# Output matrix: the first two blocks over the seven ready tiles, their low parts two merges ahead; feed-forward: convolution before the low parts, silu behind the first high part

## The chip, the cores and the metric

The program runs on one core of one Trainium2 chip. The metric is the device time in microseconds (us) of one execution, from three timed runs. Engines: PE is TensorE (matmul), DVE is VectorE, ACT is ScalarE, POOL is GpSimd, SP only issues DMAs.

## The reference, cut to what matters

A hybrid mixer block with a feed-forward part, and behind it a second block of another kind. The change touches these lines of the first block, on 256 positions and a model width of 1024:

```python
merged = (gates[:, :, 0] * (y_a @ sc_out) + gates[:, :, 1] * (y_b @ sb_out)
          + gates[:, :, 2] * (y_c @ rw_out) + gates[:, :, 3] * (y_d @ sg_out))
x = x + merged @ w_o
h = rms_norm(x, ffn_norm_g)
up = causal_dwconv(h @ w_up, conv_w)          # 3 taps, 2 * 2816 columns
gate, val = jnp.split(up, 2, axis=-1)
x = x + (jax.nn.silu(gate) * val) @ w_down
```

Everything is float32. Channels lie on partitions: a tile is 128 channels by 256 positions, and the width of 1024 is KT = 8 tiles.

## The kernel before, in words

**Weights and the split.** All weights come as one stream of blocks, 128x1024 floats (512 KB) each, through a ring of 8 slots. SP issues one DMA for each block, in order, once the slot's last reader is done. A float32 product is made of three fast ones: ACT copies a block rounded (the high part, `part_high` L254, in the feed-forward `ff_high` L1074), DVE subtracts (the low part, `part_low` L258, in the feed-forward `ff_low` L1079), and PE makes three 128x256 matmuls for each of the block's 8 pieces, 24 for a block (`three`, L263 to L265; in the feed-forward L1254 to L1256 in `up` and L1266 to L1268 in `down`).

**The merge and the output matrix (W_O).** PE first makes the branch products (`branches`, L1102), 8 blocks. For each of the 8 output tiles k DVE merges: `merge_one` (L1175, L1177), the low part of the tile before (`merged_lower(k - 1)`, L1181), two additions (L1194, L1195). ACT rounds the merged tile (L1132). Then W_O: 8 blocks m = 0..7, each a sum over the 8 merged tiles k. Its block m needs its own low part, and at m = 0 each piece k waits until tile k is merged, rounded and subtracted. DVE makes the low part of block 0 behind merge 6 (ahead of merge 7), and that of block 1 behind merge 7, ahead of `merged_lower(7)`. ACT makes the high parts of blocks 0, 1, 2 behind the roundings of tiles 3, 4, 5.

**The feed-forward.** 2816 channels are 22 tiles, each with two blocks of `w_up` (gate and value; `up`, two blocks of PE work) and one of `w_down` (`down`, one block). Two tiles (j = 0, 1) are a round of the loop; a loop of `pairs` = 10 rounds does `up` for the tiles two behind those of `down`, and two pairs of `up` stand ahead of it. Between `up` and `down` of a tile stand, on DVE, `scale_up` (L1293, twice, which also frees the PSUM banks), `convolve` (L1303 twice, L1306 four times); on ACT the silu (L1347); on POOL `hide` (L1377, L1379, L1383: product, high part, low part). `hide(i, j)` overwrites the operands of `down` of the round before, so it waits until that one has ended. In each half j of a round DVE did: low part of block 0, scale, low part of block 1, convolution, low part of block 2; ACT did three high parts and then the silu. Names below: block (n, i) is block n = 0..5 of round i; block (0, 10) and block (1, 10) are the two last ones, both of `w_down`. Nothing reorders instructions: each engine runs its own list in the written order, and the engines are tied by semaphores alone. Behind the stage stands a barrier of all engines.

## Time and profile before

| | |
|---|---|
| three timed runs | 1650.66, 1651.3, 1653.53 us; median 1651.3 |
| the profiled execution | 1651.11 us, its span 1649.3 us |
| PE busy in the span | 1587.9 us (96%) |
| DVE, ACT, POOL busy | 1180.9 us (72%), 827.8 us (50%), 435.5 us (26%) |
| mean granted clock of PE | 0.987 of full speed |

Read it so: PE is busy nearly all the time, so only the places where it stands still, or runs at a lower clock, can give time back to a change that leaves PE's work as it is. Times in rows are us from the start of the span.

### The profile page before, as it was taken

Reading aid. Unit: us, or ns where it says so; the run is one execution under the profiler, and the core shown is the slowest. Engines: PE = TensorE matmul, PEld = TensorE weight load, DVE = VectorE, ACT = ScalarE, POOL = GpSimd, SP = SyncE. Lnnn points to the kernel's source line nnn. Section 1 sums busy time; section 2 is a strip of 40 time slices with the busy share of each in tenths; the row PEclk is TensorE's granted clock in tenths of the full one; section 3 lists DMA queues with packets and bytes.
Section 4 is the critical chain, followed back from the end, with each engine's and each line's share of the span. In section 5 each row is a group of like instructions: output and inputs, shape, how many; then the busy total and the mean of one; then the engine's idle time right before and its main releaser. Section 6 shows DMA issues by size and latency. Waiting matters only on the chain. (4 is left out here: it accounts for less than half of the span.)

```text
span 1649.3 us, 34054 instructions
## 1 busy us (share of the span) xinstructions
PE 1587.9 (96%) x11842; PEld 1462.3 (89%) x11842; DVE 1180.9 (72%) x2295; ACT 827.8 (50%) x1357; POOL 435.5 (26%) x261
## 2 busy tenths in 40 slices
PE   7997999999998999999999999999999999999997
PEld 7987987999998977789999999999999888888886
DVE  5666326687786877716699996777774777777776
ACT  5364334455554463233556454555555555555554
POOL 1245540044441003456668990000000000000000
PEclk9988999999999999999999999999999999999999
DMA  8522444356663421155558775655557777777763
GB/s 288 158 62 82 127 142 128 128 180 183 186 215 118 167 77 52 59 176 197 157 170 234 217 221 165 176 177 176 182 177 223 245 241 240 232 237 238 239 227 123
DMA packets 92812, 289.56 MB, mean 176 GB/s; under 512 B 10304, under 2 KB 27072, under 8 KB 92352
## 3 DMA queue, kind: packets, MB, share of 16 engines
q1 hardware_dynamic: 92304, 287.61, 55.3%
q8 instruction: 52, 0.85, 0.2%
q10 hardware_dynamic: 432, 0.90, 0.2%
q14 instruction: 24, 0.20, 0.0%
HBM read 270.65 MB, written 17.83 MB: 175 GB/s over the span
## 5 line engine op out<-in xcount | busy, mean ns | idle before, releaser
L265 PE MATMUL psum<-arena_parts,ring_parts 128*128 128x256 f32 (+1 forms) x1856 | 525.2, 283 | 0.0
L263 PE MATMUL psum<-arena_parts 128*128 128x256 f32 (+2 forms) x1664 | 479.4, 288 | 26.5 <-DVE ring_parts L258 11.7
L2756 DVE TENSOR_TENSOR ring_parts<-ring,arena_parts 128x512 fp32r<-128x512 f32 x418 | 282.7, 690 | 112.8 <-ACT arena_parts L2550 94.8
L265 PEld LDWEIGHTS psum<-arena_parts,ring_parts 128*128 128x128 f32 x1856 | 356.0, 192 | 0.0
L263 PEld LDWEIGHTS psum<-arena_parts 128*128 128x128 f32 x1664 | 316.3, 190 | 29.5 <-DVE ring_parts L258 10.7
L264 PE MATMUL psum<-h_parts,arena_parts 128*128 128x256 f32 x1024 | 287.1, 280 | 0.0
L258 POOL TENSOR_TENSOR ring_parts<-ring,arena_parts 128x1024 fp32r<-128x1024 f32 x79 | 209.7, 2677 | 67.7 <-ACT arena_parts L254 48.8
L2519 PE MATMUL psum<-arena_parts,x_parts 128*128 128x512 f32 x512 | 201.4, 393 | 0.8 <-DVE x_parts L2783 0.8
L2520 PE MATMUL psum<-ring_parts,x_parts 128*128 128x512 f32 x512 | 201.7, 394 | 0.0
L2521 PE MATMUL psum<-arena_parts,x_parts 128*128 128x512 f32 x512 | 201.4, 393 | 0.0
L264 PEld LDWEIGHTS psum<-h_parts,arena_parts 128*128 128x128 f32 x1024 | 194.4, 190 | 0.0
L2550 ACT ACTIVATE arena_parts<-ring 128x512 fp32r<-128x512 f32 x209 | 131.5, 629 | 113.3 <-PE psum L2521 94.6
L2547 ACT ACTIVATE arena_parts<-ring 128x512 fp32r<-128x512 f32 x209 | 131.7, 630 | 69.8 <-PE psum L2521 57.3
L264 PE MATMUL psum<-arena_parts 128*128 128x256 f32 (+1 forms) x576 | 164.5, 286 | 0.0
L2519 PEld LDWEIGHTS psum<-arena_parts,x_parts 128*128 128x128 f32 x512 | 96.0, 187 | 23.6 <-DVE ring_parts L2756 1.0
L2520 PEld LDWEIGHTS psum<-ring_parts,x_parts 128*128 128x128 f32 x512 | 96.2, 188 | 22.4
L2521 PEld LDWEIGHTS psum<-arena_parts,x_parts 128*128 128x128 f32 x512 | 96.5, 188 | 21.4
L1079 DVE TENSOR_TENSOR ring_parts<-ring,arena_parts 128x1024 fp32r<-128x1024 f32 x66 | 85.7, 1301 | 38.4 <-ACT arena_parts L1074 33.7
L264 PEld LDWEIGHTS psum<-arena_parts 128*128 128x128 f32 x576 | 110.5, 192 | 0.2
L352 POOL TENSOR_TENSOR ring_parts<-ring,rounded 128x1024 fp32r<-128x1024 f32 x32 | 79.5, 2492 | 114.7 <-ACT rounded L254 114.6
L254 ACT ACTIVATE arena_parts<-ring 128x1024 fp32r<-128x1024 f32 x76 | 78.7, 1054 | 60.2 <-DMA ring<-stream 60.2
L1074 ACT ACTIVATE arena_parts<-ring 128x1024 fp32r<-128x1024 f32 x66 | 69.3, 1058 | 65.0 <-DMA ring<-stream 64.8
(547 smaller groups left out, 3270.3 us busy)
## 6 DMA issues: line engine op xcount, KB each, us to landing
ring<-stream SPq DMA_DIRECT2D x473, 512.0 KB, 3.7
kept<-arena SPq DMA_DIRECT2D x128, 128.0 KB, 2.0
arena<-kept SPq DMA_DIRECT2D x32, 512.0 KB, 4.5
arena<-first SPq DMA_DIRECT2D x1, 2144.0 KB, 16.7
arena<-second SPq DMA_DIRECT2D x1, 1632.0 KB, 6.6
x<-x_t SPq DMA_DIRECT2D x1, 1024.0 KB, 5.5
out<-arena SPq DMA_DIRECT2D x4, 256.0 KB, 2.1
arena<-last ACTq DMA_DIRECT2D x1, 512.0 KB, 3.4
```

Of the source, the lines that this page charges most:

```text
L258: ns.tensor_tensor(low[:, s, :], ring[:, s, :], high[:, s, :].bitcast(F32), ALU.subtract)\
L263: nc.tensor.matmul(dst, stationary[0], moving[0], start=first, stop=False)
L264: nc.tensor.matmul(dst, stationary[0], moving[1], start=False, stop=False)
L265: return nc.tensor.matmul(dst, stationary[1], moving[0], start=False, stop=last_one)
L352: ns.tensor_tensor(low[:, g % 4, :], ring[:, g % 4, :], rounded[:, g % 4, :].bitcast(F32), ALU.subtract)\
L1079: nc.vector.tensor_tensor(low[:, s, :], ring[:, s, :], high[:, s, :].bitcast(F32), ALU.subtract)\
L2519: mm(b, gate_high[:, q % 4, t], expert_high[:, m % 2, w], start=False, stop=False)
L2520: mm(b, gate_high[:, q % 4, t], low[:, s, w], start=False, stop=False)
L2521: ins = mm(b, gate_low[:, q % 4, t], expert_high[:, m % 2, w], start=False, stop=last_one)
L2547: nc.scalar.activation(expert_high[:, m % 2, halves[0]], ring[:, s, halves[0]], ACT.Copy)\
L2550: nc.scalar.activation(expert_high[:, m % 2, halves[1]], ring[:, s, halves[1]], ACT.Copy)\
L2756: v.tensor_tensor(low[:, s, w], ring[:, s, w], expert_high[:, m % 2, w].bitcast(F32), ALU.subtract)\
```

## The change

In W_O, PE takes blocks 0 and 1 over the tiles 0 to 6 first, then tile 7 of both, and then the blocks 2 to 7 as before. DVE makes the low part of block 0 behind merge 4 and that of block 1 behind merge 6, so that none stands behind merge 7. In the feed-forward, DVE does in each half of a round scale, convolution and then the three low parts; ACT does the silu behind the first of the three high parts. In the last round of the loop PE does both `up` and then both `down`. The last two halves are put together likewise on DVE (scale, convolution, low part) and ACT (high part, silu). The numbers of matmuls, vector operations and DMAs are the same.

```diff
+                def onto(m, ks):
+                    s, b = W_O[m], m % 4
+                    if ks[0] == 0:
+                        pe.wait_ge(full[s], (pe_at.rounds[s] + 1) * 16)
+                        pe.wait_ge(drained[b], pe_at.banks[b] + m // 4 + 1)
+                        pe.wait_ge(S("low"), o_base + m + 1)
+                    for k in ks:
+                        if m == 0 or k == KT - 1:
+                            pe.wait_ge(S("merged"), k + 1)
...
-                project(pe, W_O[:4], range(4), 1, onto(0))
-                project(pe, W_O[4:], range(4), 1, onto(4))
+                for m in range(2):
+                    onto(m, range(KT - 1))
+                for m in range(2):
+                    onto(m, range(KT - 1, KT))
+                for m in range(2, KT):
+                    onto(m, range(KT))
...
-                        if k == 6:
-                            weights_low(0)
-                weights_low(1)
+                        if k in (4, 6):
+                            weights_low(k // 2 - 2)
                 merged_lower(KT - 1)
...
-                with pe.Fori(0, pairs) as i:
+                with pe.Fori(0, pairs - 1) as i:
                     for j in range(2):
                         up(3 * j, i)
                         down(3 * j + 2, i, j)
+                for j in range(2):
+                    up(3 * j, pairs - 1)
+                for j in range(2):
+                    down(3 * j + 2, pairs - 1, j)
...
                     for j in range(2):
-                        ff_low(dve, 3 * j, i)
                         scale_up(i, j)
-                        ff_low(dve, 3 * j + 1, i)
                         convolve(i, j)
-                        ff_low(dve, 3 * j + 2, i)
-                for j in range(2):
-                    ff_low(dve, j, pairs)
-                for j in range(2):
-                    scale_up(pairs, j)
-                    convolve(pairs, j)
+                        for part in range(3):
+                            ff_low(dve, 3 * j + part, i)
+                scale_up(pairs, 0)
+                convolve(pairs, 0)
+                ff_low(dve, 0, pairs)
+                scale_up(pairs, 1)
+                convolve(pairs, 1)
+                ff_low(dve, 1, pairs)
...
                         ff_high(act, 3 * j, i)
+                        silu(i, j)
                         ff_high(act, 3 * j + 1, i)
                         ff_high(act, 3 * j + 2, i)
-                        silu(i, j)
                 for j in range(2):
                     ff_high(act, j, pairs)
-                for j in range(2):
                     silu(pairs, j)
```

DVE at the last merges, before, from the last addition of merge 6 on. L258 is a low part of W_O, L1175 and L1177 open a merge, L1181 is the low part of a merged tile, L1194 and L1195 are the additions:

```order
L1195 TENSOR_TENSOR arena<-arena 128x256
L258 TENSOR_TENSOR ring_parts<-ring,arena_parts 128x1024
L1175 TENSOR_TENSOR arena<-psum,arena 128x512
L1177 TENSOR_TENSOR arena<-psum,arena 128x512
L1181 TENSOR_TENSOR arena_parts<-arena,arena_parts 128x256
L1194 TENSOR_TENSOR arena<-arena 128x512
L1195 TENSOR_TENSOR arena<-arena 128x256
L258 TENSOR_TENSOR ring_parts<-ring,arena_parts 128x1024
L1181 TENSOR_TENSOR arena_parts<-arena,arena_parts 128x256
```

The same place of the change, from the last addition of merge 6 on (lines are 9 higher: L1184 for L1175, L1186 for L1177, L1190 for L1181, L1203 and L1204 for the additions):

```order
L1204 TENSOR_TENSOR arena<-arena 128x256
L258 TENSOR_TENSOR ring_parts<-ring,arena_parts 128x1024
L1184 TENSOR_TENSOR arena<-psum,arena 128x512
L1186 TENSOR_TENSOR arena<-psum,arena 128x512
L1190 TENSOR_TENSOR arena_parts<-arena,arena_parts 128x256
L1203 TENSOR_TENSOR arena<-arena 128x512
L1204 TENSOR_TENSOR arena<-arena 128x256
L1190 TENSOR_TENSOR arena_parts<-arena,arena_parts 128x256
L258 TENSOR_TENSOR ring_parts<-ring,arena_parts 128x1024
```

The low part between the last addition and the last L1181 is gone; the L258 ahead of merge 7 is now that of block 1, and that of block 0 stands two merges earlier.

DVE at the head of the feed-forward's loop, before (L1079 a low part, L1293 the scaling, L1303 and L1306 the convolution; the other rows are register work):

```order
L1079 TENSOR_TENSOR ring_parts<-ring,arena_parts 128x1024
L1292 REGISTER_ALU
L1293 TENSOR_TENSOR arena<-psum,scale 128x256 x2
L1078 REGISTER_ALU
L1079 TENSOR_TENSOR ring_parts<-ring,arena_parts 128x1024
L1297 ISA
L1302 ISA
L1303 ISA
L1303 TENSOR_SCALAR arena<-arena,par 128x256
```

The head of the same loop in the change, where L1305 is the scaling, L1315 and L1318 are the convolution:

```order
L1329 ISA
L1305 TENSOR_TENSOR arena<-psum,scale 128x256 x2
L1309 ISA
L1314 ISA
L1315 ISA
L1315 TENSOR_SCALAR arena<-arena,par 128x256
L1314 REGISTER_ALU
L1315 ISA
L1315 TENSOR_SCALAR arena<-arena,par 128x256
```

Scale and convolution no longer have low parts ahead of or between them.

PE where the feed-forward's loop ends, before, with what each row waits for (L1266 to L1268 are `down`):

```order
L1268 MATMUL psum<-arena_parts,ring_parts 128x256
L1273 REGISTER_ALU
L1273 COMPARE_AND_BRANCH
L1266 MATMUL psum<-arena_parts 128x256 [waits ff_hidden,low]
L1267 MATMUL psum<-arena_parts 128x256
L1268 MATMUL psum<-arena_parts,ring_parts 128x256
```

The same place of the change (L1274 to L1276 are `down`, L1262 to L1264 are `up`):

```order
L1276 MATMUL psum<-arena_parts,ring_parts 128x256
L1281 REGISTER_ALU
L1281 COMPARE_AND_BRANCH
L1262 MATMUL psum<-arena_parts 128x256 [waits low,up_taken]
L1263 MATMUL psum<-h_parts,arena_parts 128x256
L1264 MATMUL psum<-arena_parts,ring_parts 128x256
```

Behind the loop's end now stand four blocks of `up` and then four of `down`; before there were two of `down`, and the loop had one round more.

## Rows read from the trace of the kernel before

**Rows 1.** Windows; columns PE, PEld, DVE, ACT, POOL busy, clock, DMA share, GB/s

```profile
338.06:340.00 1.94, 1.94 (x9) 1.94 (x10) 1.93 (x6) 0.00 (x0) 0.00 (x0) 0.50 0.12 46
342.00:500.00 158.00, 158.00 (x1346) 158.00 (x1346) 126.45 (x209) 88.18 (x92) 66.74 (x57) 1.00 0.62 191
515.00:519.00 4.00, 4.00 (x22) 4.00 (x21) 4.00 (x8) 2.98 (x5) 0.00 (x0) 0.57 0.50 210
```

**Rows 2.** Timeline of PE, W_O: start, duration, instruction, [idle before, releaser]

```profile
288.58 0.35 PE L263 MATMUL psum<-arena_parts 128*128 128x256 f32 x1 [0.97 <-DVE ring_parts L258]
...
292.69 0.38 PE L263 MATMUL psum<-arena_parts 128*128 128x256 f32 x1 [1.40 <-DVE arena_parts L1181]
```

**Rows 3.** Timeline of PE, feed-forward: first down, two ups, last down

```profile
338.06 0.58 PE L1266 MATMUL psum<-arena_parts 128*128 128x256 f32 x1 [2.90 <-POOL arena_parts L1383]
...
342.29 0.28 PE L1254 MATMUL psum<-arena_parts 128*128 128x256 f32 x1
...
494.68 0.28 PE L1254 MATMUL psum<-arena_parts 128*128 128x256 f32 x1
...
507.32 0.36 PE L1266 MATMUL psum<-arena_parts 128*128 128x256 f32 x1 [1.19 <-POOL arena_parts L1383]
```

**Rows 4.** Timeline of DVE at the merges 5, 7 and behind

```profile
280.80 0.69 DVE L1175 TENSOR_TENSOR arena<-psum,arena 128x512 f32<-128x512 f32 x1 [0.65 <-PE psum L1102]
...
287.10 1.23 DVE L258 TENSOR_TENSOR ring_parts<-ring,arena_parts 128x1024 fp32r<-128x1024 f32 x1
288.24 0.68 DVE L1175 TENSOR_TENSOR arena<-psum,arena 128x512 f32<-128x512 f32 x1
...
289.56 0.41 DVE L1181 TENSOR_TENSOR arena_parts<-arena,arena_parts 128x256 fp32r<-128x256 f32 x1
...
291.07 1.22 DVE L258 TENSOR_TENSOR ring_parts<-ring,arena_parts 128x1024 fp32r<-128x1024 f32 x1
292.22 0.42 DVE L1181 TENSOR_TENSOR arena_parts<-arena,arena_parts 128x256 fp32r<-128x256 f32 x1
```

**Rows 5.** Timeline of ACT at the loop's start (high parts, table load, silu)

```profile
324.88 1.06 ACT L1074 ACTIVATE arena_parts<-ring 128x1024 fp32r<-128x1024 f32 x1 [2.61 <-DMA ring<-stream]
327.95 1.06 ACT L1074 ACTIVATE arena_parts<-ring 128x1024 fp32r<-128x1024 f32 x1 [2.02 <-DMA ring<-stream]
330.62 1.06 ACT L1074 ACTIVATE arena_parts<-ring 128x1024 fp32r<-128x1024 f32 x1 [1.61 <-DMA ring<-stream]
331.70 1.28 ACT L1347 ACT_TABLE_LOAD   x1
333.00 0.42 ACT L1347 ACTIVATE arena<-arena 128x256 f32<-128x256 f32 x1
```

**Rows 6.** Timeline of DVE at the loop's start (scale, convolution)

```profile
327.11 0.75 DVE L1293 TENSOR_TENSOR arena<-psum,scale 128x256 f32<-128x256 f32 x2
...
330.19 0.61 DVE L1303 TENSOR_SCALAR arena<-arena,par 128x256 f32<-128x256 f32 x2
330.71 1.70 DVE L1306 SCALAR_TENSOR_TENSOR arena<-arena,par 128x255 f32<-128x255 f32 x4
```

**Rows 7.** Timeline of POOL: the first hide and the last two

```profile
333.59 0.85 POOL L1377 TENSOR_TENSOR arena<-arena 128x256 f32<-128x256 f32 x1 [17.91 <-ACT arena L1347]
...
336.29 1.72 POOL L1383 TENSOR_TENSOR arena_parts<-arena,arena_parts 128x256 fp32r<-128x256 f32 x1
...
500.06 0.73 POOL L1377 TENSOR_TENSOR arena<-arena 128x256 f32<-128x256 f32 x1 [2.75 <-ACT arena L1347]
...
501.69 0.74 POOL L1383 TENSOR_TENSOR arena_parts<-arena,arena_parts 128x256 fp32r<-128x256 f32 x1
```

**Rows 8.** Groups of instructions by line, 342 to 500 us

```profile
L1079 DVE TENSOR_TENSOR ring_parts<-ring,arena_parts 128x1024 fp32r<-128x1024 f32 x56 | 73.6, 1315 | 32.0 <-ACT arena_parts L1074 27.7 <-DVE arena L1306 3.9
...
L1383 POOL TENSOR_TENSOR arena_parts<-arena,arena_parts 128x256 fp32r<-128x256 f32 x19 | 31.4, 1651 | 1.5
```

**Rows 9.** Timeline of ACT behind the stage's barrier

```profile
511.38 0.31 ACT L1799 ACTIVATE arena_parts<-arena 128x128 fp32r<-128x128 f32 x1 [3.87 <-PEq L1088]
```

More of the change, by code:

```diff
@@ L1104, in branches @@
                     return mm
[L1106 to L1117 removed]
+                def onto(m, ks):
[7 more added lines that the diff above has]
+                            pe.wait_ge(S("merged"), k + 1)
+                        c = slice(k * P, (k + 1) * P)
+                        ins = three(bank[b][:, 0:T], (o_high[:, s, c], low[:, s, c]), (merged_high[:, k, :], merged_low[:, k, :]),
+                                    k == 0, k == KT - 1)
+                    if ks[-1] == KT - 1:
+                        ins.then_inc(used[s], 1)
                 project(pe, range(4, 8), range(4), 1, branches)
                 project(pe, range(4), range(4), 1, branches)
[L1121 to L1122 removed]
+                for m in range(2):
[4 more added lines that the diff above has]
+                    onto(m, range(KT))
+                pe_at.advance(W_O, 1, None)
+                for b in range(4):
+                    pe_at.banks[b] += 2
             @block.scalar
```

12 lines of the change are left out of this document (removed).

## The prediction

> **What bounds the kernel now.** I read the page first: PE is busy nearly all of the span, so I looked in PE's timeline for the places where it stands still, and in the windows for a lower clock. In the loop of the feed-forward PE has no gap at all: busy 158.00 of 158 us at full clock [rows 1]. One block of 24 matmuls takes 2.82 us there, from the starts of the second `up` of round 0 and of round 9: (494.68 - 342.29) / 54 blocks [rows 3]. So the middle of the loop can give nothing; it can only lose. What is left in the two changed stages are four waits of PE: 0.97 and 1.40 us at W_O [rows 2], and 2.90 and 1.19 us at the first and the last `down` [rows 3]. The reader should also see that the 2.90 us wait has a tail: behind it the granted clock is 0.50, the lower of the two levels (1.2 for 2.4 GHz) [rows 1]. The block that starts at 338.06 ends where the next starts, 342.29 [rows 3]: 4.23 us in place of 2.82, so 1.41 us more. The shorter waits have no such tail: 0.35 and 0.38 us for their first matmul and 0.28 soon after.
>
> **W_O.** PE is done with the branches at 288.58 - 0.97 = 287.61 [rows 2] and waits for the low part of block 0, on DVE from 287.10 [rows 4]. In the change that low part stands behind merge 4. DVE has 0.65 us of idle time ahead of merge 5 and as much ahead of merge 6 [rows 4]; a low part occupies it for 1.14 us (287.10 to 288.24), so merge 5 starts 0.5 us late, merge 6 on time, and nothing is left of it. Behind merge 6 stands a low part as before, so merge 7 starts at 288.24 as before, and `merged_lower(6)` ends at 289.97 [rows 4]. PE starts block 0 at 287.6; its pieces take 2.82 / 8 = 0.353 us each, so it reaches tile 6 at 289.7 and waits about 0.3 us, to 290.05. Then: tile 6 and the seven of block 1 are 8 pieces, to 292.87. Tile 7 is needed then. It was ready at 292.64 with a low part in front; the sum is done when that low part starts, 291.07; ACT then rounds for about as long as DVE subtracts, 0.42 us, and `merged_lower(7)` ends near 291.95: 0.9 us early. Two more pieces, and block 2 starts at 293.6. Before, block 2 started at 292.69 + 9 x 0.353 = 295.9. The term is **-2.3 us**. What could be late next is the low part of block 2: now behind `merged_lower(7)`, 291.95 to 293.1, 0.5 us early; the others have 2.8 us each and cost 1.2. All that follows (residual, norm, the loads into freed slots) hangs on PE's blocks and moves along. Bounds: -1.9 (a slow first matmul, another 0.3 us of wait) to -2.4 (all of 0.97 and 1.40).
>
> **Start of the feed-forward.** The wait of 2.90 us ends with POOL's `hide(0, 0)`. Its chain was scale 327.11 [rows 6], behind a low part that waited for a DMA (its high part began at 324.88), convolution only at 330.19, behind another one, silu at 333.00 [rows 5], behind the third high part and the table load, and POOL 333.59 to 338.01 [rows 7]. In the change the chain starts when `up`(-4) ends: PE's start of this stage is two blocks before, 335.16 - 6 x 2.82 = 318.2 at the latest for the first, so 323.9 for the second. Then scale 0.4 (its first half is done by then), convolution 0.61 + 1.70 [rows 6]: 326.6. ACT: high part 324.88 to 325.94, table load 1.28, so silu at 327.3, done 327.7. POOL takes 4.42 us (333.59 to 338.01), with three of the slow form (1.72 and a gap) 5.4: done at 332.2 to 333.2. PE wants it at 338.06 - 2.90 = 335.16. So the wait is gone with 2 us in hand, and with it the low clock: **-2.90 - 1.41 = -4.3 us**. What is queued behind the moved work: low part 0 starts after the convolution, 326.7 to 327.9, wanted at 329.5; low part 1 as before behind its DMA (327.95), high part to 329.0, low to 330.3, wanted at 332.3; low part 2 (DMA at 330.62) to 332.9, wanted at 335.0. Then, on DVE now in a row, scale and convolution of j = 1 (3.1 us) to 336.1 and low part 3 to 337.3, wanted at 335.16 + 2.82 = 338.0. This is the thinnest place, 0.6 us. I take -0.1 off for it: **-4.2 us**, bounds -4.3 and -3.3 (1 us of a new, short wait there, without the clock's tail).
>
> **The middle of the loop.** The new order ties ACT and DVE in a ring: convolution, silu (0.42), second high part (1.06), second low part. A half costs DVE: 3 low parts of 1.315 [rows 8], 0.75 + 0.61 + 1.70 [rows 6], together 7.0; the ring adds silu + high part - first low part = 0.42 + 1.06 - 1.23 = 0.25 and some 0.3 of hand-overs: 7.6 us, of 8.47 that PE needs for three blocks. No wait: **0**. ACT has three high parts, a silu and a table load, 4.9 us, with both loads in one half 6.2.
>
> **End of the feed-forward.** The last `up` ends one block, 2.82 us, earlier, and so does the last convolution. But both `hide`s also wait until the `down` of the round before has ended, and these now stand behind the `up`s: they end at 500.5 and 503.3 (PE reached the last `down` at 507.32 - 1.19 = 506.13; two and one block before). `hide(10, 0)` has from 500.5 until 503.3; in the fast form it takes 2.37 us (500.06 to 502.43 [rows 7]), and fits. In the loop, though, the third operation takes 1.651 us in the mean [rows 8] in place of 0.74: POOL waits for a low part that DVE began before it. Here the low part of block (1, 10) is due at 500.8, between POOL's first and second operation; that makes one operation late by about 1.1 us, and `hide` ends at 504.1. I take a wait of 0.9 for the 1.19 that go, and none for `hide(10, 1)` (free at 504.1, done at 506.5, wanted at 507.0). DVE's way to the barrier starts 2.8 us sooner and holds one low part (1.2) more, so it ends 1.6 us sooner; PE is then the last, and ACT, which goes on at 511.38 [rows 9], moves with PE. **-0.3 us**, bounds -1.2 (no collision) and +0.7 (two collisions).
> The rule of the Trainium skill here, in "SBUF — State Buffer", section "Who interferes with whom": DVE and GpSimd share one pair of ports under an exclusive lock, a DVE instruction with two SBUF inputs takes part in it, and whoever issues first holds it to its end. The trace agrees (1.651 us against 0.74). By the lock's worst order the term is +0.7 and the sum -5.8; by engines that don't touch each other it is -1.2 and -7.7.
>
> **Sum.** -2.3 - 4.2 + 0 - 0.3 = -6.8 us, against the profiled execution's own 1651.1: 1644.3. The median of the runs is 0.2 above that execution: **1644.5 us**. Code behind the loop (96 more matmuls of `up`, 48 of `down`) replaces a round of the loop, at no cost that any row shows: W_O's 192 matmuls, written out likewise, follow each other as closely.
>
> **Rivals.**
> 1. *Another wait takes the place of the 2.90 us.* Low part 3 or 4 of round 0 comes late (their DMAs, issued at the same moment, land later than I assume, or the convolution of j = 1 is slowed), PE stands still for 2 to 3 us, and the low clock comes back. For: 0.6 us of margin, and ACT waited 2.61, 2.02 and 1.61 us for DMAs right there [rows 5]. Against: the later blocks were all in the ring by 333. Only 0.3 to 1 us of the 4.3 would be left: 1648.
> 2. *The clock behind the barrier differs.* The wait of 3.3 us behind this stage stays, and behind it PE ran at 0.57 for 4 us [rows 1], which costs (1 - 0.57) x 4 = 1.7 us. If the moved gap finds the clock otherwise, the time is 1642.8, or 1646.2 with a second such stretch. The Trainium skill, "TensorE: Matmul & The Clock Gate", section "What's actually happening", says that the number of slow matmuls after idling differs from run to run; no run here shows it yet.
> 3. *Slower: the ring of ACT and DVE becomes the loop's bound.* It needs 0.9 us more in a half than my 7.6, from collisions with POOL. From there each 0.1 us costs 2 us over 20 halves; at 8.8 us the whole gain is gone, at 9.0 the time is 1655. For: one low part delayed by POOL takes up to 0.6 us more, and there are five DVE operations to hit. Against: POOL works only 2.4 us without waiting in each half, and DVE idles for the rest.
> 4. *No difference within 0.2%*: the start's gain lost as in 1 and W_O's eaten by block 2's low part (0.5 us of margin): 1649 to 1651.
>
> **How the numbers follow.** My forecast has 0.70, with its own range 1642.8 to 1646.5 (the bounds of the terms). Rival 2's two outer values, 0.12. Rival 1, 0.08, half of it within 0.2%. Rival 3, 0.05. Rival 4, 0.05. The range: 1642.0 to 1648.0. Faster by over 0.2% (3.3 us, about what a measurement of this kernel tells from none, so below 1648.0): 0.70 + 0.12 + 0.04 = 0.86; same 0.09; slower 0.05.
>
> **What would show it.** PE's timeline after: W_O's first matmul directly behind the branches, a gap of 0.2 to 0.4 us at tile 6, none at tile 7; the first `down` 17 us behind the stage's first matmul without a gap, and the clock at 1.00 through 335 to 342; no gap in the loop; one under 1.5 us ahead of block (0, 10). DVE's waits in the loop: more on ACT for the second low part. Wrong would make it: any gap of PE in each round, or a gap with a low clock at low part 3 of round 0.

## The result, and the profile after

The changed kernel took 1639.53 us (median of four runs, 1638.52 to 1640.28). The kernel before, run beside it, took 1651.53 us (four runs, 1650.66 to 1653.53). The ratio is 0.9938, 95% interval 0.9923 to 0.9954. The profiled execution took 1640.01 us. The forecast of "faster" came true; its range, 1642.0 to 1648.0, does not hold the time.

The head of the page after, with its busy shares:

```profile
span 1638.2 us, 34047 instructions
PE 1584.2 (97%) x11842; PEld 1458.3 (89%) x11842; DVE 1183.2 (72%) x2295; ACT 826.6 (50%) x1357; POOL 443.4 (27%) x261
```

PE at W_O, timeline after. This answers to [rows 2]:

```profile
285.45 0.47 PE L263 MATMUL psum<-arena_parts 128*128 128x256 f32 x1
...
288.22 0.39 PE L263 MATMUL psum<-arena_parts 128*128 128x256 f32 x1 [0.30 <-DVE arena_parts L1190]
```

Block 0 has no wait, tile 6 is waited for 0.30 us, and tile 7 not at all. DVE at the same place, answering to [rows 4] (L1184 opens a merge, L1190 is the low part of a merged tile):

```profile
278.38 1.22 DVE L258 TENSOR_TENSOR ring_parts<-ring,arena_parts 128x1024 fp32r<-128x1024 f32 x1
279.52 0.68 DVE L1184 TENSOR_TENSOR arena<-psum,arena 128x512 f32<-128x512 f32 x1
...
289.78 0.43 DVE L1190 TENSOR_TENSOR arena_parts<-arena,arena_parts 128x256 fp32r<-128x256 f32 x1 [0.55 <-ACT arena_parts L1141]
```

The low part at 278.38 fills DVE's idle time ahead of merge 5 ([rows 4] had 0.65 us there; now there is no bracket).

The start of the feed-forward: DVE, ACT, POOL and PE after, in this order, answering to [rows 3] and [rows 5 to 7]:

```profile
319.83 0.43 DVE L1305 TENSOR_TENSOR arena<-psum,scale 128x256 f32<-128x256 f32 x1 [1.84 <-PE psum L1264]
320.70 1.69 DVE L1318 SCALAR_TENSOR_TENSOR arena<-arena,par 128x255 f32<-128x255 f32 x4
...
331.69 2.91 DVE L1079 TENSOR_TENSOR ring_parts<-ring,arena_parts 128x1024 fp32r<-128x1024 f32 x2 [0.23 <-DVE arena L1318]
```

```profile
321.65 1.28 ACT L1359 ACT_TABLE_LOAD   x1
322.95 0.42 ACT L1359 ACTIVATE arena<-arena 128x256 f32<-128x256 f32 x1
```

```profile
323.54 0.90 POOL L1388 TENSOR_TENSOR arena<-arena 128x256 f32<-128x256 f32 x1 [11.97 <-ACT arena L1359]
...
325.34 1.60 POOL L1394 TENSOR_TENSOR arena_parts<-arena,arena_parts 128x256 fp32r<-128x256 f32 x1
```

```profile
330.88 0.28 PE L1274 MATMUL psum<-arena_parts 128*128 128x256 f32 x1
...
333.71 0.28 PE L1262 MATMUL psum<-arena_parts 128*128 128x256 f32 x1
```

In words: the scaling begins when PE's `up` ends; the silu stands directly behind the table load; POOL's `hide` ends at 326.94, and PE wants it at 330.88, 3.9 us later. The first `down` takes 2.83 us (330.88 to 333.71) in place of the 4.23 of [rows 3]. Low part 3 starts at 331.69 (the first of the two in that row), takes half of 2.91 us and is wanted at 333.71, so 0.6 us are left.

Windows after, of the stretches that answer to [rows 1], with the same columns:

```profile
330.88:332.82 1.94, 1.94 (x19) 1.94 (x18) 1.72 (x3) 1.27 (x2) 0.69 (x1) 1.00 0.68 177
334.00:492.00 158.00, 158.00 (x1346) 158.00 (x1346) 135.50 (x218) 88.58 (x94) 73.12 (x56) 1.00 0.60 187
505.00:509.00 4.00, 4.00 (x22) 4.00 (x21) 4.00 (x8) 3.04 (x5) 0.00 (x0) 0.57 0.54 226
```

The clock is whole at the first `down`, the loop has no gap, and behind the barrier the granted clock is 0.57 in both profiles. Inside the loop POOL's third operation is now mostly fast (969 ns in the mean, 1651 in [rows 8]) and DVE's low part slower (1424 for 1315), at no cost to PE:

```profile
L1079 DVE TENSOR_TENSOR ring_parts<-ring,arena_parts 128x1024 fp32r<-128x1024 f32 x58 | 82.2, 1424 | 22.5 <-ACT arena_parts L1074 17.3 <-DVE arena L1318 4.4
L1394 POOL TENSOR_TENSOR arena_parts<-arena,arena_parts 128x256 fp32r<-128x256 f32 x19 | 18.4, 969 | 1.5
```

The end of the stage after, answering to the last rows of [rows 3, 7] and to [rows 9]: PE, then DVE, POOL and ACT:

```profile
495.40 0.36 PE L1274 MATMUL psum<-arena_parts 128*128 128x256 f32 x1 [0.67 <-POOL arena_parts L1394]
501.01 0.28 PE L1276 MATMUL psum<-arena_parts,ring_parts 128*128 128x256 f32 x1
503.89 0.36 PE L263 MATMUL psum<-arena_parts 128*128 128x272 f32 x1 [2.60 <-DVE arena_parts L1578]
```

```profile
491.78 1.22 DVE L1079 TENSOR_TENSOR ring_parts<-ring,arena_parts 128x1024 fp32r<-128x1024 f32 x1 [0.15 <-DVE arena L1318]
497.23 3.83 DVE L258 TENSOR_TENSOR ring_parts<-ring,arena_parts 128x1024 fp32r<-128x1024 f32 x3
```

```profile
492.06 1.56 POOL L1388 TENSOR_TENSOR arena<-arena 128x256 f32<-128x256 f32 x1 [8.53 <-PE psum L1276]
```

```profile
501.59 0.31 ACT L1810 ACTIVATE arena_parts<-arena 128x128 fp32r<-128x128 f32 x1 [4.94 <-PEq L1088]
```

Before, the same place reads (PE and DVE, rows not yet shown):

```profile
510.11 0.28 PE L1268 MATMUL psum<-arena_parts,ring_parts 128*128 128x256 f32 x1
513.68 0.36 PE L263 MATMUL psum<-arena_parts 128*128 128x272 f32 x1 [3.29 <-DVE arena_parts L1567]
```

```profile
507.58 3.50 DVE L258 TENSOR_TENSOR ring_parts<-ring,arena_parts 128x1024 fp32r<-128x1024 f32 x3
```

Before, PE ended at 510.39, DVE at 511.08, and ACT went on at 511.38 [rows 9]. After, DVE ended at 501.06, PE at 501.29, and ACT went on at 501.59. Each time ACT goes on 0.30 us behind the last engine. The two waits named "last `down`" are not at the same block: before, PE waits at the very last one, (1, 10); after, at the one before it, (0, 10), and not at (1, 10).

**Where the 11.1 us between the two spans lie.** I follow how far the profile after is ahead of the one before at the same matmul. It is ahead by 1.81 us when the branches start (258.06 against 256.25), before anything that was changed. At the feed-forward's first `up` it is 4.11 (317.91 against 313.80), at the second `up` of round 0 it is 8.58 (342.29 against 333.71), at the next stage's first matmul 9.79 (513.68 against 503.89). So: **W_O 2.30, start 4.47, end 1.21**, together 7.98 us. (The brackets make a wait too small by 0.16 us: they count from the end of a matmul of 0.28 us, while in a stream the next one starts 0.12 us behind the last. So the 2.90 us wait costs 3.07, 20.15 us from the first `up` to the first `down` in place of 17.08, and the 2.07 us by which the waits of W_O differ, with one wait fewer, make 2.23 of the 2.30.) In a later stage, with the same code in both kernels, come 1.5 us more.

### The profile page after: what moved, and what is told of

It reads as the page before. It is cut to its first block and busy times, and to the rows that moved or that the text cites. A ratio compares the mean times of both kernels' runs of the same rounds, so it can differ in the third digit from the quotient of the medians.

```text
span 1638.2 us, 34047 instructions
## 1 busy us (share of the span) xinstructions
PE 1584.2 (97%) x11842; PEld 1458.3 (89%) x11842; DVE 1183.2 (72%) x2295; ACT 826.6 (50%) x1357; POOL 443.4 (27%) x261
## 5 line engine op out<-in xcount | busy, mean ns | idle before, releaser
L258 POOL TENSOR_TENSOR ring_parts<-ring,arena_parts 128x1024 fp32r<-128x1024 f32 x79 | 210.3, 2684 | 65.3 <-ACT arena_parts L254 46.8
L254 ACT ACTIVATE arena_parts<-ring 128x1024 fp32r<-128x1024 f32 x76 | 78.8, 1054 | 63.1 <-DMA ring<-stream 62.9
L1079 DVE TENSOR_TENSOR ring_parts<-ring,arena_parts 128x1024 fp32r<-128x1024 f32 x66 | 92.2, 1404 | 25.1 <-ACT arena_parts L1074 19.4
L1262 PE MATMUL psum<-arena_parts 128*128 128x256 f32 x352 | 98.9, 281 | 0.0
```

Source lines behind the costliest of these rows:

```text
L258: ns.tensor_tensor(low[:, s, :], ring[:, s, :], high[:, s, :].bitcast(F32), ALU.subtract)\
L1079: nc.vector.tensor_tensor(low[:, s, :], ring[:, s, :], high[:, s, :].bitcast(F32), ALU.subtract)\
L1262: mm(b, high[:, s, w], h_high[:, k, :], start=k == 0, stop=False)
```

## Experiments

The kernel before ran beside the others in every comparison; with the runs of the first comparison and those of `before_again` it has 109 runs: median 1648.6 us, 1644.35 to 1655.36. Ratios are against the runs of the same comparison. The waits are PE's, read from its timeline; "last `down`" is the wait at block (0, 10) or (1, 10), whichever has one, and "next stage" that of the next stage's first matmul.

| kernel | median us (range, runs) | ratio [95%] | W_O | first `down` | last `down` | next stage |
|---|---|---|---|---|---|---|
| before | 1651.53 (1650.66-1653.53, 4) | | 0.97 + 1.40 | 2.90 | 1.19 | 3.29 |
| before_again | 1647.84 (1644.91-1652.55, 10) | 0.9994 [0.9982, 1.0007] | 0.96 + 1.40 | 2.94 | 1.11 | 3.27 |
| wo_lows_only | 1651.08 (1647.92-1654.05, 8) | 1.0011 [0.9995, 1.0026] | 0.30 + 1.42 | 2.57 | 0.88 | 3.30 |
| wo_pe_only | 1648.71 (1646.58-1653.5, 8) | 1.0005 [0.9991, 1.0019] | 0.97 + 1.16 | 2.49 | 1.18 | 3.29 |
| wo_only | 1647.14 (1644.46-1650.01, 10) | 0.9987 [0.9974, 1.0] | 0.31 | 3.02 | 0.87 | 3.29 |
| ff_dve_only | 1646.2 (1644.54-1649.28, 10) | 0.9976 [0.9966, 0.9986] | 0.97 + 1.40 | 0.70 | 0.68 | 3.82 |
| ff_peel_only | 1650.09 (1645.25-1653.46, 12) | 1.001 [0.9996, 1.0024] | 0.97 + 1.40 | 3.03 | 0.26 | 3.29 |
| ff_only | 1645.06 (1641.69-1647.26, 10) | 0.9974 [0.9961, 0.9988] | 1.00 + 1.37 | none | 0.67 | 2.60 |
| no_peel | 1644.68 (1643.56-1646.88, 7) | 0.9972 [0.9961, 0.9984] | 0.31 | none | 0.69 | 3.83 |
| after | 1639.53 (1638.52-1640.28, 4) | 0.9938 [0.9923, 0.9954] | 0.30 | none | 0.67 | 2.60 |
| after_again | 1640.47 (1638.46-1642.59, 4) | 0.9941 [0.9918, 0.9964] | 0.30 | none | 0.67 | 2.60 |
| after_third | 1641.53 (1637.66-1644.82, 9) | 0.9955 [0.9939, 0.997] | 0.30 | none | 0.76 | 2.60 |
| race_fix | 1642.86 (1638.33-1646.37, 12) | 0.9963 [0.9951, 0.9975] | 0.30 | none | 0.85 | 2.60 |
| before_race_fix | 1649.21 (1645.97-1656.04, 12) | 1.0006 [0.9994, 1.0019] | 0.97 + 1.39 | 2.69 | 1.01 | 3.29 |
| tail_tuned | 1641.58 (1639.25-1643.65, 6) | 0.9957 [0.9942, 0.9971] | 0.30 | none | 0.57 | 2.92 |
| both | 1641.53 (1640.87-1644.76, 5) | 0.9957 [0.9943, 0.9972] | 0.31 | none | none | 2.87 |

**The kernel before and the changed kernel, again.** No edit.

> The kernel before, unchanged, profiled once more. The change gave 11.1 us between the two profiled executions, of which 8.0 lie between the start of the branch products and the first matmul of the next stage (2.30 W_O, 4.47 start of the feed-forward, 1.21 its end), 1.8 lie ahead of the changed stages and 1.3 behind them. Theory A (chance): the 1.8 ahead and the 1.3 behind are from where the low-clock stretches fall and from single waits that differ between executions; then this second profile of the same kernel starts the branch products somewhere else than 258.06, between 256 and 259, and the four waits of PE in the changed stages (0.97, 1.40, 2.90, 1.19) are there to 0.2 us. Theory B (systematic): they belong to the change; then the branch products start at 258.06 to 0.3 us again. Time 1651.5 within 1.5.

> The changed kernel, profiled once more. Theory A: the start of the branch products moves by up to 2 us against 256.25, while the stretch from there to the next stage's first matmul stays at 503.89 - 256.25 = 247.6 us to 0.5. Theory B: it starts at 256.25 to 0.3 again. Time 1639.5 within 1.5, ratio 0.9927.

> The changed kernel, nothing altered. So far two comparisons of four runs each gave it 1639.5 and 1640.5 us, and four kernels that differ from it by a wait or an order at the end gave 1641.5 to 1642.9. Theory S (the change is worth what its stretches show, 6.8 to 8.0 us, and the rest of the first result of 12.0 us is chance, in the few runs of the kernel before above all): median 1640.5 to 1642 us, 6.8 to 8 us under the kernel before of the same chip. Theory T (the change does bring 11 us or more, through something behind the two stages that the profile pairs do not show steadily): median under 1639.5 us. The stretches in the profile: start of the branches to first up block 55.8 to 57.6 us, then 17.1, 169.9, no wait at the first down block, 0.67 us at the last, 2.60 us for the next stage.

In `before_again` theory A holds: the branches start at 257.09, and the four waits are there to 0.1 us; its time, 1647.84, misses the 1650 to 1653 that I expected. In `after_again` they start at 258.64, and from there to the next stage it is 247.63 us, as expected.

The changed kernel has 17 runs in all: median 1640.5 us, mean 1640.7, 1637.66 to 1644.82. Against 1648.6 (mean 1649.0) that is 8.1 us by the medians and 8.3 by the means, with standard deviations of 2.0 and 2.3 us over the runs, so some 1 us either way. Theory S holds: the change is worth about what its stretches show (7.98), and the 12.0 us of the first comparison hold some 4 us of chance, 2.9 of them in its four runs of the kernel before (1651.53 for 1648.6). The later comparisons ran on three different chips and gave the kernel before 1648.5, 1648.9, 1648.6 and 1647.8, so between those the chip matters little; the chip of the first comparison isn't known.

**W_O alone, and its two halves.** `wo_only` is the whole of it; `wo_lows_only` is the first diff, `wo_pe_only` the second:

```diff
-                        if k == 6:
-                            weights_low(0)
-                weights_low(1)
+                        if k in (4, 6):
+                            weights_low(k // 2 - 2)
```

```diff
...
-                project(pe, W_O[:4], range(4), 1, onto(0))
-                project(pe, W_O[4:], range(4), 1, onto(4))
+                for m in range(2):
+                    onto(m, range(KT - 1))
+                for m in range(2):
+                    onto(m, range(KT - 1, KT))
+                for m in range(2, KT):
+                    onto(m, range(KT))
```

> W_O's part of the change alone (PE's split of blocks 0 and 1, DVE's low parts two merges ahead), the feed-forward as before. Theory A: 2.3 us less than before, ratio 0.9986; PE's waits at W_O are one of 0.3, those of the feed-forward 2.90 and 1.19 as before. Theory B (a part of the change also pulls the stages around it): more than 3.5 us less.

> The kernel before, and of the change only DVE's low parts of W_O two merges ahead; PE takes block 0 over all eight tiles first, as before. By the ledger of the prediction PE starts block 0 at once behind the branches (0.97 gone), waits 0.3 at tile 6 and then 1.5 in place of 1.40 at tile 7, because it comes there earlier and merged_lower(7) is only 0.7 earlier: the stretch from the branches' first matmul to the feed-forward's first is 0.7 us shorter (59.1 for 59.8). If the two halves of W_O's edit simply added, it would be about half of 2.3.

> The kernel before, and of the change only PE's split of W_O's blocks 0 and 1; DVE's low parts stand where they stood. Block 0 waits 0.97 as before; block 1 then waits for its own low part, which is ready at 292.3, 1.2 us after block 0's tile 6 is done; tile 7 waits no more. Gain 0.3 to 0.4 us. Together with the other half 1.1 us, where the whole edit gave 2.30: the theory says that each half alone runs into the wait that the other one removes. A rival is that PE's split alone carries it: then 1.4 us or more.

PE's waits in W_O, both of `wo_lows_only` and then the second of `wo_pe_only`:

```profile
289.78 0.39 PE L263 MATMUL psum<-arena_parts 128*128 128x256 f32 x1 [0.30 <-DVE arena_parts L1181]
291.82 0.58 PE L263 MATMUL psum<-arena_parts 128*128 128x256 f32 x1 [1.42 <-DVE arena_parts L1181]
```

```profile
292.56 0.36 PE L263 MATMUL psum<-arena_parts 128*128 128x256 f32 x1 [1.16 <-DVE ring_parts L258]
```

(The `onto` of `wo_pe_only` is that of the change.) The low parts alone take the waits from 2.37 to 1.72 us: block 0 starts at once, and PE is then so much earlier at tile 7. PE's order alone brings 2.13: PE now wants block 1's low part ahead of tile 7, and in DVE's old order it is not made yet. Together 0.31. The gain of 2.06 us is over twice the sum of the halves (0.65 + 0.24): each order needs the other. The medians don't tell the halves from nothing, and hardly `wo_only`; the waits of one profile each show this, not the times.

**The feed-forward, alone and in parts.** `ff_only` has all its edits and no edit of W_O. `ff_dve_only` is only this:

```diff
                     for j in range(2):
-                        ff_low(dve, 3 * j, i)
                         scale_up(i, j)
-                        ff_low(dve, 3 * j + 1, i)
                         convolve(i, j)
-                        ff_low(dve, 3 * j + 2, i)
-                for j in range(2):
-                    ff_low(dve, j, pairs)
-                for j in range(2):
-                    scale_up(pairs, j)
-                    convolve(pairs, j)
+                        for part in range(3):
+                            ff_low(dve, 3 * j + part, i)
+                scale_up(pairs, 0)
+                convolve(pairs, 0)
+                ff_low(dve, 0, pairs)
+                scale_up(pairs, 1)
+                convolve(pairs, 1)
+                ff_low(dve, 1, pairs)
```

`no_peel` is the changed kernel less PE's new order in the last round, `ff_peel_only` the kernel before with that order only:

```diff
-                with pe.Fori(0, pairs) as i:
+                with pe.Fori(0, pairs - 1) as i:
...
+                for j in range(2):
+                    up(3 * j, pairs - 1)
+                for j in range(2):
+                    down(3 * j + 2, pairs - 1, j)
```

> The feed-forward's part of the change alone, W_O as before. Theory A: 4.47 + 1.21 = 5.7 us less than before, ratio 0.9966. Theory B: over 7 us less.

> The kernel before, and of the change only DVE's order in the feed-forward (scale, convolution, then the low parts; in the last two halves too). ACT still does the first silu behind three high parts, PE's order is as before. Theory A (the first silu's place on ACT decides): the third high part waits for a DMA that lands 12.7 us behind the stage's first matmul, silu ends at about 15.5, hide at 20, so PE's wait of 2.90 at the first down stays at 2.4 to 2.9 although the convolution is done 6 us earlier. Theory B (DVE's order decides): the wait is gone. At the stage's end DVE's order alone shortens the last wait from 1.19 to 0.9 or less.

> The changed kernel without PE's new order at the end of the feed-forward (up and down alternate in all ten rounds, as before). The last up then ends one block later and the hides don't wait for a down that stands late: hide(10, 0) is done in time; the last down waits for hide(10, 1), whose chain is second half of the scale, convolution, silu, three operations of POOL, the first of them behind the low part of block (1, 10): 6.6 us against 5.64 of PE's work, so a wait of 0.5 to 1.0 at the last down in place of the 0.67 one block earlier. PE's new order at the end is then worth nothing, to 0.3 us. The start of the feed-forward is as in the changed kernel, no wait at the first down.

> The kernel before with only TensorE's new order in the last round of the feed-forward (both up blocks, then both down blocks); VectorE and ScalarE keep their orders, and the output matrix is as before. Theory A (the next stage starts 0.30 us behind the last engine, which is VectorE by 0.69 us before, so what brings VectorE's last convolution forward brings the next stage forward): the first down block still waits 2.5 to 2.9 us, the wait of 1.19 us at the last down blocks shrinks to 0 to 0.7, the next stage's first matmul waits 2.60 in place of 3.29 us, and the local gain is 0.7 to 1.9 us. Theory B (that order is worth something only with VectorE's new order, whose convolutions then stand ahead of the low parts): both waits as before, 1.1 to 1.2 and 3.3 us, and no gain. Medians will hardly tell 1 us; the waits in the profile decide.

The first `down` in `ff_dve_only`, PE, then ACT and POOL ahead of it:

```profile
335.29 0.39 PE L1266 MATMUL psum<-arena_parts 128*128 128x256 f32 x1 [0.70 <-POOL arena_parts L1383]
```

```profile
332.07 0.42 ACT L1347 ACTIVATE arena<-arena 128x256 f32<-128x256 f32 x1
```

```profile
332.66 0.88 POOL L1377 TENSOR_TENSOR arena<-arena 128x256 f32<-128x256 f32 x1 [17.55 <-ACT arena L1347]
334.44 0.79 POOL L1383 TENSOR_TENSOR arena_parts<-arena,arena_parts 128x256 fp32r<-128x256 f32 x1
```

I had expected 2.4 to 2.9 us here, since the silu still stands behind the third high part. It does, at 332.07. But DVE then has no low part in the way while POOL works, all three of POOL's operations are fast (DVE has scale and convolution there), and `hide` takes 2.57 us (332.66 to 335.23) in place of the 4.42 of [rows 7]. So DVE's order brings 2.2 of the 2.9 us, most of it by leaving POOL alone, and ACT's order the last 0.7 and the margin.

The end of the stage in `no_peel`, and in `ff_peel_only`: DVE's last low parts, then PE:

```profile
499.99 3.50 DVE L258 TENSOR_TENSOR ring_parts<-ring,arena_parts 128x1024 fp32r<-128x1024 f32 x3
```

```profile
506.08 0.36 PE L263 MATMUL psum<-arena_parts 128*128 128x272 f32 x1 [3.83 <-DVE arena_parts L1574]
```

```profile
508.32 3.50 DVE L258 TENSOR_TENSOR ring_parts<-ring,arena_parts 128x1024 fp32r<-128x1024 f32 x3
```

```profile
508.06 0.36 PE L1266 MATMUL psum<-arena_parts 128*128 128x256 f32 x1 [0.26 <-POOL arena_parts L1387]
514.41 0.57 PE L263 MATMUL psum<-arena_parts 128*128 128x272 f32 x1 [3.29 <-DVE arena_parts L1571]
```

Add the last two columns of the table, last `down` and next stage. The kernel before 4.48, DVE's order alone 4.50, PE's order alone 3.55, both 3.27 us. DVE's order alone saves 0.5 at the last `down` and gives it back at the barrier, which DVE holds. PE's order alone saves 0.9 at `hide` and nothing at the barrier. Only together is PE the last engine, and the gain 1.2. The wait at `hide` is not steady, though: six profiles with the old end have sums of 4.16 to 4.48 (mean 4.33), the five that have the change's end 3.27 to 3.45 (mean 3.32). So the gain is 1.0 us in the mean; its 0.69 at the barrier is there in every one (3.27 to 3.30 against 2.60). I had expected of `no_peel` that its order is worth nothing; it was worth 1.2. In `ff_peel_only` theory A is right about the first wait (0.26) and theory B about the second (3.29).

**A stage that nobody changed.** Some 200 us later, in the mixing stage, the profile after gained 1.5 us. DVE, POOL and PE before:

```profile
772.36 2.79 DVE L2226 TENSOR_TENSOR arena_parts<-arena,arena_parts 128x512 fp32r<-128x512 f32 x1
```

```profile
772.21 2.38 POOL L258 TENSOR_TENSOR ring_parts<-ring,arena_parts 128x1024 fp32r<-128x1024 f32 x1 [0.17 <-ACT arena_parts L254]
```

```profile
775.20 0.39 PE L263 MATMUL psum<-arena_parts 128*128 128x256 f32 x1 [1.25 <-DVE arena_parts L2226]
```

POOL starts 0.15 us ahead of DVE, and DVE's 0.69 us become 2.79. After, DVE starts 0.1 us ahead, takes 0.69, and PE has no wait. So I made POOL wait, in the kernel before and in the changed one:

```diff
                 for m in range(16):
+                    if m == 15:
+                        pool.wait_ge(S("mixed"), 4)
                     part_low(pool, nc.gpsimd, mix_high, to_split[m][0], mix_base + m + 1)
```

> Everything of the changed kernel, and one more wait in the mix stage: GpSimd does its sixteenth low part only behind VectorE's last mixed low part (L2237 there). Theory R (the two engines share a way to SBUF, and who starts first there decides by 0.1 to 0.2 us): VectorE's last mixed low part takes 0.69 us, GpSimd's cast of 2.4 us starts behind it, TensorE has no wait of 1.25 us at that place, the stretch L2120 to L2430 takes 70.2 us. The changed kernel has 70.2 us in both its profiles already, so its median stays where it is, within 1 us of 1640; what can shrink is the share of runs that lose the race (those of 1642 and more). Theory N (the 2.75 us has another cause, such as a late transfer): the stretch is as often 71.8 as 70.2 us, or GpSimd's later start moves a wait of 0.6 us to TensorE behind it.

> The kernel before with the same one wait of GpSimd in the mix stage, nothing else. In both profiles of the kernel before GpSimd's cast started first (VectorE's L2226 then took 2.79 us) and the stretch L2120 to L2430 took 71.7 and 71.8 us. Theory R: with the wait L2226 takes 0.69 us, the stretch takes 70.2 us, and the median is 0.7 to 1.5 us under that of the kernel before (1.5 if it loses the race in each execution, less if it loses in half of them). That is then the size of what the changed kernel got from the mix stage by luck of its timing. Theory N: 71.8 us as before, and no difference.

In `before_race_fix`, DVE and PE a little later:

```profile
771.58 0.69 DVE L2228 TENSOR_TENSOR arena_parts<-arena,arena_parts 128x512 fp32r<-128x512 f32 x1
...
784.53 2.37 DVE L2232 SCALAR_TENSOR_TENSOR arena_parts<-x,par,arena_parts 128x256 fp32r<-128x256 f32 x1 [2.93 <-ACT arena_parts L2192]
```

```profile
791.02 0.36 PE L263 MATMUL psum<-arena_parts 128*128 128x256 f32 x1 [1.39 <-DVE arena_parts L2232]
794.38 0.39 PE L263 MATMUL psum<-arena_parts 128*128 128x256 f32 x1 [0.65 <-DVE arena_parts L2232]
```

Theory R is right about the place: 0.69 us, and the wait of 1.25 is gone. It is wrong about the time. 13 us on DVE's 0.49 us operation met POOL's work and took 2.37, but it does so in all sixteen profiles (2.34 to 2.37). What differs is when it starts. DVE waited 2.93 us for ACT, and ACT for a block of weights that came late:

```profile
783.04 1.06 ACT L254 ACTIVATE arena_parts<-ring 128x1024 fp32r<-128x1024 f32 x1 [6.16 <-DMA ring<-stream]
```

That is 59.75 us behind the start of the stretch; in the twelve profiles whose stretch takes 70.2 to 70.4 us it is 57.2 to 58.2. PE waited 1.39 us there (0.97 to 1.00 in the other profiles) and 0.65 once more, and the stretch took 71.6 us in place of 71.75: 0.2 us, and 1649.21 us against 1648.6. Why the block came late no run shows; holding POOL back isn't shown to be the reason, since with the same wait `race_fix` had it at 58.2. In `race_fix` the stretch took 70.4, as good as in the changed kernel, and its median is not below it. Of the sixteen profiles twelve have 70.2 to 70.4 us and four 71.6 to 71.9 (`before`, `before_again`, `wo_only`, `before_race_fix`). In `tail_tuned`, `after_third` and `after_again` DVE's operation was slow too (2.80, 2.77 and 2.78) and cost nothing, because the one ahead of it was fast (0.43 in place of 2.52). In these profiles two such delays in a row make PE wait, and one does not.

**A version with the end put in another order.** In the changed kernel, both last low parts go ahead of the last scale and convolution, nine small operations move ahead of the loop, and the next stage's three low parts go behind the last `hide`. `both` adds the wait in the mixing stage:

```diff
                 ff_low(dve, -1)
+                gain_1, gain_2 = (par[:, at[n]:at[n] + KT] for n in ("final_norm_g", "norm1_g_2"))
+                dve.wait_ge(S("meta_in"), 16)
+                v.tensor_tensor(both_g, gain_1, gain_2, ALU.mult)
...
                 ff_low(dve, 0, pairs)
+                ff_low(dve, 1, pairs)
                 scale_up(pairs, 1)
                 convolve(pairs, 1)
-                ff_low(dve, 1, pairs)
-                gain_1, gain_2 = (par[:, at[n]:at[n] + KT] for n in ("final_norm_g", "norm1_g_2"))
-                dve.wait_ge(S("meta_in"), 16)
-                v.tensor_tensor(both_g, gain_1, gain_2, ALU.mult)
...
+                dve.wait_ge(S("ff_hidden"), 2 * pairs + 4)
```

> The changed kernel with VectorE's work around the last half of the feed-forward in another order: both low parts of the last two blocks ahead of the last half's scale and convolution, and the nine operations on gains and eps (6.6 us of VectorE's queue) ahead of the loop in place of behind it; the three low parts for the next stage behind the last hide. Theory A (the wait of 0.67 us at the last two blocks is for GpSimd's hide, which stands behind VectorE's convolution; the barrier follows the last engine by 0.30 us, and that is now TensorE): the barrier stays 0.30 us behind TensorE, the last down blocks start no later, the stretch from the start of the branches to the next stage's first matmul is 0 to 0.7 us shorter than in the changed kernel (247.6 us when it was 248.2 less the early low clock), and the nine operations cost nothing ahead of the loop if VectorE has 6 us there, which it does not quite have: if the first scale comes late by x us, the first down block waits x. Theory B (VectorE's chain low part, scale, convolution decides the start of the loop): the first down block waits 3 to 6 us again and the kernel is slower by as much. I hold A for the end at 0.6 and B for the start at 0.4.

> The changed kernel with the wait in the mix stage and VectorE's new order around the end of the feed-forward together. If each does what its theory says, 1639.5 to 1640.5 us: the sum of the two, which is 0 to 0.7 us for the end, and no lost race. If the nine operations ahead of the loop make the first down block wait (theory B of the kernel with the new order alone), 1643 to 1646 us.

The end of the stage on DVE and PE in `both`:

```profile
502.49 3.50 DVE L258 TENSOR_TENSOR ring_parts<-ring,arena_parts 128x1024 fp32r<-128x1024 f32 x3 [5.04 <-POOL arena_parts L1396]
```

```profile
508.58 0.56 PE L263 MATMUL psum<-arena_parts 128*128 128x272 f32 x1 [2.87 <-DVE arena_parts L1580]
```

Theory A was right about the start: the nine operations cost nothing ahead of the loop (no wait at the first `down`). But my own wait for `hide` let DVE start its last low parts only at 502.49, so DVE is again the last engine, by 0.27 us (2.87 for 2.60). The last two columns are 3.49 us in `tail_tuned` and 2.87 in `both`, for 3.27 in the changed kernel. Neither median is below the changed kernel's, and `both` missed its 1639.5 to 1640.5.

## Why the prediction was right in direction and its range missed

**W_O: right.** -2.3 forecast, 2.30 measured between the same matmuls of the profiled pair (and again 2.30 between `ff_only` and `after_again`, from the branches' start to the first `up`); block 0 without a wait, 0.30 us at tile 6, nothing at tile 7, merge 5 later by what DVE's idle time didn't cover. `merged_lower(7)` waited 0.55 us for ACT's rounding, where the working has 0.42, and ended at 290.21, still 0.8 us ahead of PE.

**Start of the feed-forward: right in mechanism, 0.3 us short.** -4.2 forecast, 4.47 measured. The chain ran as worked out, with 3.9 us in hand rather than 2, since POOL needed 3.40 us and not 5.4; low part 3 had the 0.6 us of margin, and no new wait took its place (rival 1 did not come). Of the 0.3, 0.1 had been taken off for low part 3, and 0.16 is what the bracket of 2.90 leaves out. Of the 4.3, though, only the 2.90 is the wait's own. The 1.41 of low clock behind it is not always there: `before_again` waited 2.94 us, and the windows of the two kernels' first `down` read

```profile
338.00:342.00 4.00, 3.94 (x22) 3.94 (x23) 3.22 (x7) 1.89 (x3) 1.35 (x2) 0.63 0.07 29
```

```profile
336.88:341.00 4.12, 4.12 (x35) 4.12 (x36) 3.16 (x7) 2.06 (x3) 1.44 (x2) 1.00 0.02 6
```

The same wait, once with a granted clock of 0.63 behind it, once at 1.00. Of the seven kernels that wait 2.49 to 3.03 us there, five have the low clock behind it (their first `down` takes 4.2 to 4.5 us) and two don't (2.93 us each). I had counted this as certain.

**The loop: right.** 158.00 of 158 us busy; rival 3 did not come.

**End of the feed-forward: this is the step that failed.** "-0.3 us" was forecast, 1.21 measured in the pair (1.0 in the mean over the profiles), at the bound of -1.2 that I had given to an end without a collision, though there was one. Two sizes were off. The wait at the last `down` came to 0.67, not 0.9: POOL's slow operation was the first (1.56 for 0.73), 0.8 us late and not 1.1. And the barrier: I worked out that DVE "ends 1.6 us sooner; PE is then the last", and left it at that. I did not read that DVE had held the barrier 0.69 us past PE's end before. That 0.69 is the difference of the next stage's waits, 3.29 - 2.60, and is missing from the sum, which put the barrier at nothing. `no_peel` and `ff_peel_only` bear it out: in neither is PE last, and neither has 2.60.

**The sum and its base.** With this the change's own part is 8.0 in the profiled pair, not 6.8 us; from 1651.3 that gives 1643.3, still inside the range. What took the result out of it is the other step that failed: "The median of the runs is 0.2 above that execution". I treated 1651.3, the median of three runs, as the kernel's time within a few tenths; over 109 runs it is 1648.6, and single runs are spread over 11 us. 1648.6 less 8.0 is 1640.6, and the 17 runs of the changed kernel give 1640.5. That they meet to 0.1 us is luck: with the low clock at the first `down` in five of seven and the end's mean of 1.0, the same stretches are worth 2.3, 4.1 and 1.0, together 7.4 us over all profiles, against 8.1 from the runs with 1 us either way.

The forecast's own range doesn't come out of its terms either: their bounds add up to -7.9 and -4.5 us, which is 1643.4 to 1646.8 and not 1642.8 to 1646.5.

**Rival 2** names one of the causes of this spread, at nearly its price: `after_again` shows no low clock behind the barrier, `after` 0.57, and the stretch differs by 1.5 us (1.7 in the rival). It was too small for the whole because there are several such causes.

**What stays open.** The parts' medians are lower than their waits: `wo_only` gives -1.4 against the kernel before beside it and `ff_only` -3.4, together 4.8, the whole change 8.1, while their waits add as they should, with 2.06 and 1.21 us less at the same places. Their intervals hold the ratios that the waits forecast (0.9986 and 0.9966), so this is not shown to be more than chance. How often each low-clock stretch comes may itself depend on the change; no run here shows that.

One more cause of the spread can be placed. The last 635 us, with the same code, take 638.6 to 638.9 in five of the sixteen profiles (`before_again`, `ff_dve_only`, `no_peel`, `after_again`, `before_race_fix`) and 634.8 to 635.7 in the others. The difference lies in the last stage, spread evenly over some 350 us of 128x512 matmuls. `after`, then `no_peel`:

```profile
1400.00:1500.00 100.00, 100.00 (x434) 81.23 (x433) 74.16 (x146) 56.72 (x109) 0.00 (x0) 1.00 0.71 235
```

```profile
1400.00:1500.00 100.00, 100.00 (x431) 80.37 (x430) 73.22 (x144) 56.40 (x108) 0.00 (x0) 1.00 0.71 235
```

PE has no gap and the whole clock in both, yet one starts a matmul every 0.2311 us and the other every 0.2333. Kernels with and without the change are among the five. Why, no run here shows.

## What to carry to other kernels

At a barrier, write down for every engine when it ends before and after the change; the time moves with the last one, and an order that moves only one of two engines can save nothing or a part, and both together more than the sum. Before pricing a change of 0.5%, know the spread of single runs: here the median of three runs was 2.7 us above that of 109, as much as a part of the change is worth. List a profile's low-clock stretches and take them out before explaining anything else. When an engine is held back at one place, read the whole stretch behind it: here the gain was gone 13 us on, by a transfer that came late.

## What the runs showed of the hardware that I had not expected

**The clock behind a gap is a lottery with several draws.** At the start of the branches PE has stood still for 3.06 or 3.09 us in every profile. The six microseconds behind it, in `race_fix`, `after` and `after_third`:

```profile
258.90:264.90 6.00, 6.00 (x28) 5.30 (x29) 2.16 (x4) 4.54 (x5) 0.00 (x0) 1.00 0.87 314
```

```profile
256.30:262.30 6.00, 6.00 (x20) 5.06 (x21) 0.64 (x1) 4.49 (x5) 0.00 (x0) 0.72 0.85 306
```

```profile
258.00:264.00 6.00, 5.98 (x15) 4.81 (x16) 0.00 (x0) 4.56 (x5) 0.00 (x0) 0.52 0.86 311
```

Granted clock 1.00, 0.72 and 0.52; the stretch from there to the first `up` took 55.9, 57.5 and 58.7 us, with the same 0.30 us of waits. So this draw is worth 0 to 2.8 us. The one behind the barrier is worth up to 1.5 in the changed kernel (12.2 or 13.7 us for the same stretch), the one behind the first `down` 1.4 in the kernel before, and one some 200 us behind the mixing stage 1.5 (206.6 or 208.1 us for the stretch around it, in kernels with the same code there). The Trainium skill says in "TensorE: Matmul & The Clock Gate", section "What's actually happening", that the number of slow matmuls varies from run to run; these profiles agree, and show that their number can also be none.

**Two engines at the same memory.** In the mixing stage a DVE subtraction of 0.69 us takes 2.75 to 2.92 when a POOL subtraction of 2.4 us has started 0.01 to 0.20 us before it (six profiles), and POOL's takes 2.73 to 2.94 when it starts 0.01 to 0.23 us behind DVE's (four). The Trainium skill, "SBUF — State Buffer", section "Who interferes with whom", has this as an exclusive lock that whoever issues first holds for its whole instruction; the times agree. What I had not expected is that 0.1 to 0.2 us of start time decides over 1.25 us of PE's, where the operation ahead was slow too.

**PE at full clock and without a gap is not always equally fast.** In the last stage it starts a matmul every 0.2311 us in eleven profiles and every 0.2333 in five, with no value between, at a granted clock of 1.00: some 3.5 us over the stage.
